# Token rows of the routed experts kept in HBM by quarter rows: one load of 128 partitions in place of four of 32

## What is computed

```
logits = xt @ w_router
top_logit, top_idx = lax.top_k(logits, 2)
gates = softmax(top_logit)
# rows are grouped by expert, xs = the tokens' rows in that order
hid = silu(xb @ w_gate[e]) * (xb @ w_up[e])      # D 1024 -> 3584
yb  = hid @ w_down[e]                            # 3584 -> 1024
y[token] += yb[row] * gate[row]
```

## Time and profile before

| | us |
|---|---|
| median of 3 runs | 1381.68 |
| lowest and highest of them | 1376.52, 1383.98 |
| the profiled execution | 1385.25 |
| its span in the trace | 1383.4 |
| granted TensorE clock, mean | 0.987 of full |

### The profile page before, as it was taken

One profiled execution on the slowest core, in us unless ns is written; L12 is line 12 of the kernel. 1 busy time (PEld: TensorE's weight loads), 2 busy tenths in 40 slices (PEclk: granted clock), 3 DMA queues, 4 the chain that ended last, 5 costly groups with the idle time before them and its releaser, 6 DMA issues.

```text
span 1383.4 us, 32475 instructions
## 1 busy us (share of the span) xinstructions
PE 1316.3 (95%) x14601; PEld 774.3 (56%) x14601; DVE 360.1 (26%) x500; ACT 243.2 (18%) x364; POOL 42.0 (3%) x35
## 2 busy tenths in 40 slices
PE   6998999999899699999999999999999999999998
PEld 6997899988777334634633533443452353354344
DVE  5874555554875501001101101101100100110111
ACT  5463544443742100000000000000000000000000
POOL 0001000000000100000000000000000000002400
PEclk9999999999999899999999999999999999999999
DMA  9972455565421896999999999999999999999996
GB/s 324 355 238 61 149 183 183 184 212 183 182 92 61 347 371 237 388 415 351 410 421 401 387 419 415 376 417 407 376 413 420 366 409 421 389 388 418 412 379 235
DMA packets 128838, 442.52 MB, mean 320 GB/s; under 512 B 9588, under 2 KB 56004, under 8 KB 112324
## 3 DMA queue, kind: packets, MB, share of 16 engines
q1 hardware_dynamic: 122736, 424.75, 80.8%
q10 hardware_dynamic: 4820, 11.53, 2.3%
q0 software_dynamic: 1152, 4.19, 0.8%
HBM read 434.12 MB, written 12.08 MB: 323 GB/s over the span
## 4 chain that ended last, share of the span: by engine, by line
PE 73%; DMA 17%; DVE 4%; SPq 2%; ACT 2%; issue 2%; ACTq 0%; POOL 0%; DVEq 0%; POOLq 0%
PE bank L1689 31%; PE bank L1701 14%; DMA dn<-in_moe_w_down 8%; PE bank L1332 8%; PE bank L1334 8%; PE bank L1333 8%; DMA raw<-in_moe_w_gate 7%; DMA raw<-in_moe_w_up 2%; SPq L430 1%; PE bank L1589 1%; PE bank L1537 1%; SPq L459 1%; PE bank L1470 1%; DVE w_lo L831 0%; ACT w_hi L564 0%
## 5 line engine op out<-in xcount | busy, mean ns | idle before, releaser
L1689 PE MATMUL bank<-raw,xT 128*32 128x512 f32 (+1 forms) x4608 | 441.3, 540 | 6.5 <-DMA raw<-in_moe_w_up 3.1
L1689 PEld LDWEIGHTS bank<-raw,xT 128*32 128x32 f32 x4608 | 152.9, 110 | 287.6 <-issue 251.6
L1701 PE MATMUL bank<-dn,hidT 128*32 128x256 f32 x5376 | 292.8, 379 | 13.0 <-DMA dn<-in_moe_w_down 12.9
L1701 PEld LDWEIGHTS bank<-dn,hidT 128*32 128x32 f32 x5376 | 178.1, 110 | 129.1 <-DMA dn<-in_moe_w_down 24.0
L831 DVE TENSOR_TENSOR w_lo<-raw,w_hi 128x2048 fp32r<-128x2048 f32 x62 | 141.7, 2291 | 112.5 <-ACT w_hi L564 112.4
L1303 DVE TENSOR_TENSOR e_hid<-e_silu,bank 128x512 f32<-128x512 f32 (+1 forms) x48 | 26.9, 616 | 552.6 <-PE bank L1689 552.6
L1689 PE MATMUL bank<-up_more,xT 128*32 128x384 f32 (+1 forms) x1536 | 151.2, 540 | 2.8 <-DMA up_more<-in_moe_w_up 1.8
L1332 PE MATMUL bank<-ht_hi,w_hi 128*128 128x256 f32 x480 | 137.1, 286 | 5.1 <-DVE w_lo L904 2.7
L1333 PE MATMUL bank<-ht_lo,w_hi 128*128 128x256 f32 x480 | 136.5, 284 | 0.0
L1334 PE MATMUL bank<-ht_hi,w_lo 128*128 128x256 f32 x480 | 136.4, 284 | 0.0
L564 ACT ACTIVATE w_hi<-raw 128x2048 fp32r<-128x2048 f32 x62 | 118.5, 1915 | 51.4 <-PE bank L1334 51.4
(11 more groups left out here) (257 smaller groups left out, 818.5 us busy)
## 6 DMA issues: line engine op xcount, KB each, us to landing
dn<-in_moe_w_down SPq DMA_DIRECT2D x112, 1024.0 KB, 15.4
raw<-in_moe_w_gate SPq DMA_DIRECT2D x48, 1024.0 KB, 18.1
raw<-in_moe_w_up SPq DMA_DIRECT2D x48, 1024.0 KB, 16.9
raw<-in_moe_w_gate SPq DMA_DIRECT2D x48, 768.0 KB, 13.5
raw<-in_moe_w_up SPq DMA_DIRECT2D x48, 768.0 KB, 11.0
up_more<-in_moe_w_gate SPq DMA_DIRECT2D x16, 1024.0 KB, 26.0
up_more<-in_moe_w_up SPq DMA_DIRECT2D x16, 1024.0 KB, 16.6
raw<-in_hgrn_w_in SPq DMA_DIRECT2D x15, 1024.0 KB, 12.7
```

Of the source, the lines that this page charges most:

```text
L1689: ins = nc.tensor.matmul(out_banks[j][GTOK * c:GTOK * c + GTOK, 0:w], xT[:, j, kt, :], chunk[:, c], start=kt == 0, stop=kt == KT - 1)
L1701: ins = nc.tensor.matmul(banks[6 + j // 2][GTOK * c:GTOK * c + GTOK, 256 * (j % 2):256 * (j % 2) + 256], hidT[sup][:, g, m, :], dn[:, i % ...
```

## The change

The table in HBM keeps its bytes but is addressed as 5632 quarter rows of 1 KB (`x_rows`). Within an item's block of 384 quarter rows, the order is now group, quarter, token: quarter c of row t of group j stands at 128j + 32c + t. So the tile `xr`, whose content and use don't change, is filled by one DMA over 128 partitions with three pieces of 1 KB each, where four DMAs filled 32 partitions each with three pieces of 1 KB.

For this, each row is scattered in four pieces, with 16 indirect DMAs (128 pieces of 1 KB each) in place of four. Their places need the number of whole groups of 32 rows ahead of `pos`: DVE compares `pos` with the 44 multiples of 32 (`passed`), sums the hits (`block_of`), adds 96 times that to `pos`, and adds 0, 32, 64 and 96 for the quarters (`slot`). These four operations stand behind the three transposes of item 0; the cast of `slot`, which stood ahead of `sel`, is gone. Two small operations that fill `steps` and `quarters` stand ahead of the router's wait. The results' store and the fetch of the results still use whole rows, at the same places.

```diff
@@ build_program
     slot_rows = nc.dram_tensor("slot_rows", [ROWS, D], f32, kind="Internal").ap()
+    x_rows = slot_rows.rearrange("r (q d) -> (r q) d", q=4)
...
-        slot = sb(ctx, "slot", [P, TT, 2], u32)
+        slot = sb(ctx, "slot", [P, TT, 2, 4], u32)
+        steps = sb(ctx, "steps", [P, 44])
+        quarters = sb(ctx, "quarters", [P, 4])
+        passed = sb(ctx, "passed", [P, TT, 2, 44])
+        block_of = sb(ctx, "block_of", [P, TT, 2])
@@ SyncE
             def load_rows(n):
-                rows = slot_rows[bass.ds(n * CAP, CAP), :].rearrange("(j t) d -> t j d", t=GTOK)
-                for c in range(4):
-                    sp.dma_start(xr[GTOK * c:GTOK * c + GTOK, :, :], rows[:, :, 256 * c:256 * c + 256]).then_inc(xr_loaded, 16)
+                sp.dma_start(xr[:, :, :], x_rows[bass.ds(n * 4 * CAP, 4 * CAP), :].rearrange("(j p) d -> p j d", p=P)).then_inc(xr_loaded, 16)
             for t in range(TT):
                 for i in range(2):
-                    sp.wait_ge(spread[t][i], 16)
+                    sp.wait_ge(spread[t][i], 16 * 4)
             load_rows(1)
@@ GpSimd
             for t in range(TT):
                 for i in range(2):
-                    to = bass.IndirectOffsetOnAxis(ap=slot[:, t, i:i + 1], axis=0)
-                    nc.gpsimd.indirect_dma_start(out=slot_rows, out_offset=to, in_=xs[:, t, :], in_offset=None).then_inc(spread[t][i], 16)
+                    for c in range(4):
+                        to = bass.IndirectOffsetOnAxis(ap=slot[:, t, i, c:c + 1], axis=0)
+                        nc.gpsimd.indirect_dma_start(out=x_rows, out_offset=to, in_=xs[:, t, 256 * c:256 * c + 256],
+                                                     in_offset=None).then_inc(spread[t][i], 16)
@@ VectorE
+            nc.vector.tensor_scalar(steps[:, :], const[:, K_IOTA:K_IOTA + 44], float(GTOK), float(GTOK), MUL, ADD)
+            nc.vector.tensor_scalar(quarters[:, :], const[:, K_IOTA:K_IOTA + 4], float(GTOK), None, MUL)
...
-            nc.vector.tensor_copy(slot[:, :, :], pos[:, :, :]).then_inc(slots_ready, 1)
...
+            then(nc.vector.tensor_tensor(passed[:, :, :, :].rearrange("p t i s -> p (t i) s"), every_choice(pos[:, :, :]).to_broadcast([P, 2 * TT, 44]),
+                                         steps[:, :].unsqueeze(1).to_broadcast([P, 2 * TT, 44]), ALU.is_ge))
+            then(nc.vector.tensor_reduce(block_of[:, :, :].rearrange("p t i -> p (t i)"), passed[:, :, :, :].rearrange("p t i s -> p (t i) s"), AX.X, ADD))
+            then(nc.vector.scalar_tensor_tensor(out=block_of[:, :, :], in0=block_of[:, :, :], scalar=float(CAP), in1=pos[:, :, :], op0=MUL, op1=ADD))
+            nc.vector.tensor_tensor(slot[:, :, :, :].rearrange("p t i c -> p (t i) c"), every_choice(block_of[:, :, :]).to_broadcast([P, 2 * TT, 4]),
+                                    quarters[:, :].unsqueeze(1).to_broadcast([P, 2 * TT, 4]), ADD).then_inc(slots_ready, 1)
...
-                dve.wait_ge(xr_loaded, n * 64 + 64)
+                dve.wait_ge(xr_loaded, n * 16 + 16)
```

## The result

| us | before | after |
|---|---|---|
| median, 20 runs each | 1383.45 | 1375.47 |
| lowest and highest | 1376.07, 1387.67 | 1371.37, 1380.89 |
| the profiled execution | 1385.25 | 1371.37 |
| its span | 1383.4 | 1369.5 |

The ratio is 0.9949, with a 95% interval of 0.9936 to 0.9961: 7.1 us faster, where 17.3 were forecast (the medians differ by 8.0). The time lies inside the stated range of 1357 to 1377, but the gain is only about 40% of the one forecast. The change's gain was there in full, and almost two thirds of it were lost again in item 0, at a place that the prediction had priced at nothing.

The account below looks back on a forecast made before the run. DMA engines were taken as the bound from item 2 on, PE close behind. Dips 17.2 us plus DVE 0.1 make 17.3 us, from 1381.68 to 1364.4 us (chance 0.76, own range 1359 to 1370); stated range 1357 to 1377.

Parts of the forecast that it names:

- The bound and the place of the loss: From item 2 on DMA engines bound the kernel; 28.1 us lost, mostly in row-load stretches at 281 to 333 GB/s.
- The price of the dips: Bandwidth drops while each item's rows load, items 1 to 7: 18.4 us at 410 GB/s, 17.2 us to be saved.
- The 348 GB/s of the early loads: Rate of 1 KB-piece loads over 128 partitions at 10 to 50 us, taken for the new row load: 1.13 us each.
- rival 2: Only the row load's own bytes get faster, 200 to 348 GB/s: 5.8 us saved, 1375.9 us; chance 0.07.
- The SyncE queue: Three of four row-load issues go, some 1.4 us an item; valued at nothing because full DMA queues cover it.
- PE takes it all: PE gives the whole 17.2 us: items then cost DMA 109.5 us, PE 108.4, with 28.1 us of room.
- The scatter: Item 0: POOL issues 16 indirect DMAs, 20.2 us, from 479.3 to 499.5, landed by 508.4; cost nothing, cover 27 us.
- So 0: Cost given to the scatter's writes in item 0's up stage, with 5.4 us as the worst, absorbed.
- term for slow 1 KB writes: Scatter's 2.1 MB in 2048 packets during item 0's up stage: 5.1 us at 410 GB/s, 10.5 at 200.
- PE waits in item 0's up stage: Sign against the forecast: it would say the scatter's 1 KB writes cost more than allowed.
- rivals 2 and 3: Only the rows' own bytes faster, 1375.9 us, chance 0.07; or SyncE queue issues the cause, 1372.3 us, chance 0.05.

Follow-up runs that it names:

- the kernel with 64-byte rows: Changed kernel with each of the 16 scatters writing 64 bytes a row, not 1 KB, into its own table; ratio 0.9935 to the kernel before.

## Why the prediction was wrong

- **The bound and the place of the loss**: right. The windows named the stretches, and the dips in them are gone, with the DMA engines as busy as before.
- **The price of the dips**, 18.4 us, of which 17.2 were to go: right, 17.7 in the profile and 17.4 or more in all. The 348 GB/s of the early loads was the right row for the new load; what remains of a dip is under 0.2 us, as worked out.
- **The figure of the Trainium skill** ("SBUF — State Buffer", "Door 1: The DMA port swizzle") gave 5.9 us for the slow bytes alone, and rival 2 had that size. The ports fit the trace as a mechanism, since only the loads over 32 partitions dip, though no run parts the 32 partitions from the four DMAs. As a price the page's figure is a third of the measured one: it prices the transfer itself, and four fifths of the loss (14.7 of 18.6 us of packet time) were in the weights' packets that moved beside it.
- **The SyncE queue**: right to value it at nothing. The first down load now follows the row load after 0.65 us (650.08 to 650.73) in place of 2.23, and the packets' extra time, 18.6 us, covers the gain of 17.7 without it. No run changed the issues alone. The chain had shown these issues on its path, and they were not the cause.
- **PE takes it all**: right, with items 1 to 6 at 108.4 to 110.4. The prediction had 109 to 110 from item 2 on; two more items stayed at the floor, which fits a lead in the buffers that lasts longer when each item eats less of it. Item 7 is at 114.4, 2.8 us less than before, the size of its dip; the 6 us that it stays above the floor are something else, which the prediction did not tell apart.
- **The scatter**: this is the step that failed. Its own course was nearly as told: 16 made 1.27 us apart (1.26), begun at 473.6 in this profile, 1.3 us behind the last transpose, its last packet at 495.0, long before SP wants them. (The prediction counted 2048 packets of 1 KB; the trace has 768, of which 512 carry 4 KB, in 167 ns each, as fast as the weights' packets of that size. So its term for slow 1 KB writes isn't there at all.) It was priced at nothing because bytes, queue and the waits on it were all covered, and the sum has it as "So 0". The term left out is what the making itself does to PE where the hole occurs: 11.1 us in the result's profile. The prediction did say that PE waits in item 0's up stage would speak against it, but put them down to the cost of 1 KB writes, which the kernel with 64-byte rows rules out.
- **The trace of before could not show this term.** It has four scatters in a row, 5 us, over at 477.3, before PE's loop begins at 478.25, and the hole came 11.1 us after the first. The prediction took four seen in flight as a sign for 16 and bounded only their landing. On four of the five chips of the experiments the term is in fact nothing, and the forecast (1364.4 of 1381.68, 0.9875) lies inside both intervals of the unaltered changed kernel there.
- **The time in the range is luck.** 1375.5 us lies above the forecast's own 1359 to 1370. The range reached up to 1377 so as to take in rivals 2 and 3, and neither of these is what happened.

## What to carry to other kernels

Where a DMA-bound stream loses bandwidth while its engines stay busy, look for a transfer over few partitions in that stretch (in several small DMAs here; the two weren't separated), and count what it does to its neighbours' packets as well as its own bytes. When a change turns a few indirect DMAs into a long row of them, its cost is not only its place in the queues: look at PE's idle time put down to "issue" beside the row, and don't extend a short row's harmlessness to a long one. The same program gained 0.6% in one set and 1.6% in another, so a disputed part and its rival belong in the same set, on the same chip.

## What the runs showed that was not expected

- While 16 indirect DMAs were made without a break, PE fell from 120 matmuls in 12 us to 22, waiting for nothing recorded, with the clock at 1.00; the same program in another set did 119 in the same 12 us.
- The hole begins 11.1 us after the first indirect DMA of the row, whether that is made at 473.6 or at 483.1, and whether the row moves 2.1 or 0.13 MB.
- A load of 0.393 MB over 32 partitions at a time cost 2.8 us in most items beyond its bytes, most of it in the weights' packets beside it (4 KB in 213 ns in place of 164); over 128 partitions it cost under 0.2 us.
